# A state-space kernel matrix is stored and read back as a Toeplitz matrix: from the SyncE queue to GpSimd

## The chip, the cores and the metric

One core of a Trainium2 chip runs the whole program. The metric is the device time of one execution in microseconds (us); lower is better. All times come from runs on the chip and from one execution that the hardware profiler recorded.

## What is computed

The program is one inference step of a two-layer trunk over 264 tokens (256 of a prompt, 8 single-token samples), with shared weights, in f32. Each layer joins three branches fed by one projection: an S5 state space, a retention branch with a 128 x 256 state for each head and sample, and a convolution. A feed-forward part follows: dense in layer 0, eight experts in layer 1.

```python
z = u @ w_in
s5_out, s5_re, s5_im = s5_branch(z[..., OFF_S5:OFF_Q], ...)      # h = lbar*h + bbar*u ; y = Re(C h) + D u
ret_out, ret_state   = retention_branch(...)
conv_out, conv_state = conv_branch(...)
merged = gate_a*(s5_out @ s5_proj) + gate_b*(ret_out @ ret_proj) + gate_c*(conv_out @ conv_proj)
x = x + merged @ w_out
x = x + swiglu(rmsnorm(x))          # layer 0;  layer 1: top 2 of 8 experts
```

## The kernel before

**How the S5 part is done.** The 256 prompt tokens are cut into 32 chunks of S = 8. Inside a chunk the recurrence is a fixed 8 x 8 block-Toeplitz matrix of 16 x 16 blocks for each of 32 groups. TensorE makes the eight different blocks (tiles `kk`), ScalarE copies them into 16 partitions of `s5m` (L1263), and VectorE adds the skip term (L1758, semaphore `kmat_ready`). To become Toeplitz, these 16 partitions are stored to a scratch tensor in HBM, `kscr` (L618, 256 KB), and read back eight times, each time shifted by one block, into another 16 partitions of `s5m` (L624, 8 x 256 KB, semaphore `toep_in`). The tiles `y` (L910, L914) read the matrix. Before them TensorE waits for `h_ready`, which VectorE gives at the end of the sweep over the 32 chunks (L1674 to L1680), and for `toep_in` (L902).

**How weights arrive.** Dense weights come in chunks of 512 KB (eight 128 x 128 blocks) into a ring of five slots. SyncE (SP) issues them in order (L595); chunk n waits until TensorE is done with chunk n - 5. ScalarE makes the high part of a chunk (L1150), VectorE the low part (L1518), and TensorE uses three matmuls for each block (L684 to L686). ScalarE and VectorE do this up to two chunks ahead, but in program order with their other work: `full(key)` first splits the chunks up to the key's own plus two, and only then waits for the key.

**The order around the change.** On TensorE: gates `gg` 0 and 1, transposes `win`, `kk`, `si`, sample state 0, then `gg` 2 to 7 with the sample states 1, 2 and 3 behind `gg` 3, 4 and 6, then `y`, `gs` 0, sample state 4. In layer 0 `gg` 2 to 7 use chunks 30 to 35, `gs` 0 and 1 use 36 and 37 (layer 1: 182 to 187, 188 and 189). VectorE's update of sample state 3 stands behind the low part of chunk 36 (layer 1: 188), and the last step of the sweep behind that update. On SP the store and the eight loads stand between the issues of chunks 34 and 35 (layer 1: 186 and 187): SP waits for `kmat_ready`, stores, waits until the store has landed, issues the eight loads, and goes on to chunk 35.

**GpSimd (POOL)** makes the powers of the state matrix (`turns`, up to L2236) and then, for the sample states 0 to 7, waits for VectorE's update and stores the state (L2240, 512 KB). Between these it loads the states 4 to 7 (L2245). GpSimd's DMAs run on a queue of their own (q0, software), SP's on q1 (hardware).

Of the kernel before, what the change touches and what calls it, by code (L numbers as in the profile page):

```python
# [29 lines left out]
DEPTH = 2  # L30
G = 32
GP = 16
GJ = G // 2
S = 8
# [14 lines left out]
RING = 5  # L49
# [160 lines left out]
def chunk_of_tile():  # L210

    last, b = {}, 0
    for key, blocks in tile_order():
        b += blocks
        last[key] = (b + CH - 1) // CH - 1
    return last
# [13 lines left out]
def build(nc, a):  # L230
# [13 lines left out]
    CHUNK_OF = chunk_of_tile()  # L244
    PART = part_order()

    with ExitStack() as ctx:
        start_of = {}

        def sb(name, shape, dt=F):  # L250
            start_of[name] = -(-nc.sbuf_base // 32) * 32
            return ctx.enter_context(nc.sbuf_tensor(name, shape, dt))
# [6 lines left out]
        def sem(name):  # L259
            return ctx.enter_context(nc.semaphore(name))  # L260
# [6 lines left out]
        s5m = sb("s5m", [P, 15648])  # L267
# [147 lines left out]
        def weights(c, of):  # L415

            s = c % RING
            return of[:, s * CH * P:(s + 1) * CH * P]
# [10 lines left out]
        def slot(c, of):  # L429

            s = c % MRING
            return of[:, s * 2048:(s + 1) * 2048]
# [17 lines left out]
        kscr = nc.dram_tensor("kscr", [GP, (2 * S - 1) * G * GP], F, kind="Internal").ap()  # L450
# [28 lines left out]
        kmat_ready = sem("kmat_ready")  # L479
        dd_ready = sem("dd_ready")  # L480
        kscr_out = sem("kscr_out")
        toep_in = sem("toep_in")
        bc_in = sem("bc_in")
        zero_out = sem("zero_out")
# [55 lines left out]
        def out_of(key):  # L540

            return evicted[PLACE[key] % NBANK], PLACE[key] // NBANK + 1
# [33 lines left out]
        @block.sync  # L576
        def _(sp):
            sp.dma_start(lam[:, :, :], a["lam"]).then_inc(lam_in, 16)
            sp.dma_start(xT[:, :, :], a["xT"]).then_inc(x_in, 16)
            for n in range(2):  # L580
                sp.dma_start(weights(n, ring), a["weights"][n]).then_inc(loaded[n], 16)
            loads = [(vecs[:, :], a["vecs"]), (kdec[:, :, :], a["kdec"]),
                     (ident[:, :], a["ident"]), (tri[:, :], a["tri"]), (iota[:, :], a["iota"]),
                     (dskip[:, :, :], a["dskip"]), (router[:, :, :], a["router"])]
            for dst, src in loads:
                sp.dma_start(dst, src).then_inc(consts_in, 16)
            sp.dma_start(rope, a["rope"]).then_inc(table_in, 16)


            zg = zscr.rearrange("(g p) t -> p g t", p=GP)  # L590
            for n in range(2, N_CHUNKS):
                if n >= RING:

                    sp.wait_ge(mm_done, CHUNK_DONE[n - RING])
                sp.dma_start(weights(n, ring), a["weights"][n]).then_inc(loaded[n % RING], 16)  # L595
                for l in range(DEPTH):
                    if n == CHUNK_OF[(l, "v", 3)] + RING:

                        sp.wait_ge(*out_of((l, "k", 3)))
                        sp.dma_start(decay, a["decay"]).then_inc(table_in, 16)  # L600
                for l in range(DEPTH):
                    step = n - RING - CHUNK_OF[(l, "k", 0)]
                    if step == 0:

                        sp.wait_ge(zscr_out, 16 * (l + 1))
                        sp.wait_ge(xin_zero, 1)
                    if 0 <= step < S // 2:
                        for i in (2 * step, 2 * step + 1):
                            sp.dma_start(xin[i * GP:(i + 1) * GP, :, 0:NC], zg[:, :, i * NC:(i + 1) * NC]).then_inc(xin_in, 16)
                    if step == S // 2:  # L610
                        sp.dma_start(xin[0:GP, :, NC:NC + NS], zg[:, :, SEQ:T]).then_inc(xin_in, 16)
                        sp.dma_start(xin[P - GP:P, :, NC + NS:NC + 2 * NS], zg[:, :, SEQ:T]).then_inc(xin_in, 16)
                for l in range(DEPTH):
                    if n == CHUNK_OF[(l, "gg", 1)] + RING:

                        before = (S - 1) * G * GP
                        sp.wait_ge(kmat_ready, l + 1)
                        sp.dma_start(kscr[:, before:before + S * G * GP], s5m[0:GP, 0:S * G * GP]).then_inc(kscr_out, 16)  # L618
                        sp.wait_ge(kscr_out, 16 * (l + 1))
                        if l == 0:  # L620
                            sp.wait_ge(zero_out, 16)
                        for s in range(S):
                            lo = (S - 1 - s) * G * GP
                            sp.dma_start(s5m[s * GP:(s + 1) * GP, 0:S * G * GP], kscr[:, lo:lo + S * G * GP]).then_inc(toep_in, 16)  # L624
                if n == CHUNK_OF[(0, "gl", 0)] + RING:

                    sp.wait_ge(h_ready, 1)
                    sp.dma_start(rope, a["rope"]).then_inc(table_in, 16)


            sp.wait_ge(mm_done, DONE[(DEPTH - 1, "ps", KD - 1)])
            sp.wait_ge(merged, 16 * (DEPTH - 1) + KD)
            sp.wait_ge(hstate_out, 32 * DEPTH)
            for s in range(MRING):
                sp.dma_start(slot(s, s5m), a["experts"][s]).then_inc(mloaded[s], 16)
            l = DEPTH - 1
            sp.wait_ge(mm_done, DONE[(l, "xt", 5)])
            sp.dma_start(g_fin, a["gfin"]).then_inc(g_fin_in, 16)
            for i in range(3):
                lo, n = UT[i]  # L640
                n += CAP * (i == 2)
                sp.wait_ge(u_tok_ready, i + 1)
                sp.dma_start(u_rows[lo:lo + n, :], utok[0:n, i, :]).then_inc(u_rows_in, 16)
            sp.wait_ge(items_ready, 1)
            items = sp.value_load(items_t[0:1, 0:1], min_val=NEXP, max_val=3 * NEXP)
            with sp.Fori(0, items * TURNS - 1) as q:
                for s in range(MRING):

                    sp.wait_ge(mm_done, q * MRING + MM_BASE + s + 1)
                    row = ((q + 1) % (NEXP * TURNS)) * MRING + s  # L650
                    sp.dma_start(slot(s, s5m), a["experts"][bass.ds(row, 1)].rearrange("o p x -> (o p) x")
                                 ).then_inc(mloaded[s], 16)

            for s in range(AHEAD):
                sp.wait_ge(mm_done, items * E_CHUNKS + MM_BASE - MRING + s + 1)
                sp.dma_start(slot(s, s5m), a["experts"][s]).then_inc(mloaded[s], 16)


            sp.wait_ge(rows_added, items * 16 + 48)
            for i in range(3):  # L660
                lo, n = UT[i]
                sp.dma_start(xfin[0:n, i, :], x_rows[lo:lo + n, :]).then_inc(x_back[i], 16)
            for i in range(3):
                lo, n = UT[i]
                sp.wait_ge(x_final, i + 1)
                sp.dma_start(a["y"][lo:lo + n, :], xfin[0:n, i, :]).then_inc(y_out, 16)
            sp.wait_ge(y_out, 48)
# [1441 lines left out]
        def _(pool):  # L2109
# [36 lines left out]
            before = (S - 1) * G * GP  # L2146
# [6 lines left out]
            for l in range(DEPTH):  # L2153
# [74 lines left out]
                def more_turns(n):  # L2228

                    product([turns[:, r, :, n:2 * n] for r in range(2)], [turns[:, r, :, 0:n] for r in range(2)],  # L2230
                            [turns[:, r, :, n - 1:n].broadcast_to([P, GJ, n]) for r in range(2)], spare[:, :, 0:n])

                first_turns()
                for n in (1, 2, 4, 8, 16):
                    more_turns(n)
                pool.tensor_copy(spare[:, 0:1, 0:1], damp[:, 0:1].unsqueeze(2)).then_inc(turns_ready, 1)  # L2236
                for b in range(NS):
                    pool.wait_ge(*out_of((l, "oa", b)))
                    pool.wait_ge(*out_of((l, "ob", b)))
                    pool.dma_start(a["ret_s"][l, b], states[b % 4]).then_inc(s_out[b % 4], 16)  # L2240
                    if 1 <= b <= 4:
                        c = b - 1
                        pool.wait_ge(mm_done, DONE[(l, "os", c)])
                        pool.wait_ge(s_out[c], 16 * (2 * l + 1))
                        pool.dma_start(states[c], a["sret"][l, c + 4]).then_inc(s_in[c], 16)  # L2245
# [20 lines left out]
            for i in range(3):  # L2266
                lo, n = UT[i]
# [162 lines left out]
```

## Time and profile before

| what | us |
|---|---|
| three timed runs | 1957.0, 1957.76, 1958.45 (median 1957.76) |
| span of the profiled execution | 1954.9 |
| busy: TensorE | 1848.1 (95%) |
| busy: VectorE | 1544.7 (79%) |
| busy: ScalarE | 1195.4 (61%) |
| busy: GpSimd | 347.2 (18%) |
| moved by DMA | 527.5 MB, 270 GB/s in the mean |

Busy times are those of the profiled execution. Its program spans 1954.9 us; some 2.9 us of the timed median lie around the span. A busy TensorE is not TensorE at full rate: the granted clock says how fast it ran.

### The profile page before, as it was taken

The numbers are of one execution on the slowest core, as the hardware profiler recorded it, in microseconds if no ns is written. First come the engines' busy times: TensorE is split into PE (matmuls) and PEld (weight loads), VectorE is DVE, ScalarE is ACT, GpSimd is POOL, SyncE is SP. The second block draws the span as 40 slices with busy tenths as digits, with TensorE's granted clock in tenths as the row PEclk, the third lists the DMA queues.
The fourth block names the chain that finished last, engine by engine and source line by source line (L and its number), as shares of the span: only waits on it lengthen the run. The fifth ranks groups of instructions, "written<-read, shape, count | busy, mean of one in ns | idle before, by whom it ended". The sixth has DMA issues, their size and how long they took to land.

```text
span 1954.9 us, 31463 instructions
## 1 busy us (share of the span) xinstructions
PE 1848.1 (95%) x11751; PEld 1559.0 (80%) x11751; DVE 1544.7 (79%) x1758; ACT 1195.4 (61%) x1274; POOL 347.2 (18%) x449
## 2 busy tenths in 40 slices
PE   7788989899998998999899999999999999999995
PEld 6687889899998987999577777777777777777774
DVE  6986887666646967875699888898888988888886
ACT  4235545454434455454677777777777777777765
POOL 7974100069900030000000000000000000000000
PEclk8999999999999998999899999999999999999998
DMA  5447554455554656546599999999999999999996
GB/s 188 138 151 187 185 173 153 161 176 184 177 191 160 206 103 216 188 153 242 203 372 375 379 363 364 364 364 380 372 368 362 364 390 356 372 363 363 389 356 243
DMA packets 106786, 527.50 MB, mean 270 GB/s; under 512 B 22103, under 2 KB 23543, under 8 KB 62743
## 3 DMA queue, kind: packets, MB, share of 16 engines
q1 hardware_dynamic: 97303, 494.52, 69.6%
q0 software_dynamic: 8336, 30.63, 5.2%
q8 instruction: 63, 1.03, 0.2%
q10 hardware_dynamic: 1056, 1.08, 0.2%
q14 instruction: 28, 0.23, 0.0%
HBM read 505.69 MB, written 20.50 MB: 269 GB/s over the span
## 4 chain that ended last, share of the span: by engine, by line
PE 52%; DVE 4%; issue 3%; ACT 3%; DMA 2%; DVEq 0%; ACTq 0%; POOL 0%; POOLq 0%
PE bank L684 16%; PE bank L686 16%; PE bank L685 16%; DVE s5m_parts L2049 2%; PE bank L1091 1%; ACT zone_parts L1451 1%; DMA ring<-in_weights 1%; PE bank L1036 1%; DVE ring_parts L1518 0%; PE bank L717 0%; DMA s5m<-in_experts 0%; DVE s5m L1538 0%; PE bank L1123 0%; DMA x_rows<-work 0%; DVE zone L1649 0%
## 5 line engine op out<-in xcount | busy, mean ns | idle before, releaser
L2049 DVE TENSOR_TENSOR s5m_parts<-s5m,ring_parts 128x2048 fp32r<-128x2048 f32 x228 | 519.3, 2286 | 71.7 <-ACT ring_parts L1451 70.2
L1451 ACT ACTIVATE ring_parts<-s5m 128x2048 fp32r<-128x2048 f32 x228 | 432.2, 1917 | 89.5 <-DMA s5m<-in_experts 89.2
L1518 DVE TENSOR_TENSOR ring_parts<-ring,ring_parts 128x1024 fp32r<-128x1024 f32 x238 | 312.4, 1319 | 179.5 <-ACT ring_parts L1150 178.7
L684 PE MATMUL bank<-uT_parts,ring_parts 128*128 128x264 f32 x1312 | 386.9, 295 | 52.7 <-DVE ring_parts L1518 36.6
L685 PE MATMUL bank<-uT_hi,ring_parts 128*128 128x264 f32 x1312 | 380.6, 290 | 0.0
L686 PE MATMUL bank<-uT_hi,ring_parts 128*128 128x264 f32 x1312 | 379.9, 290 | 0.0
L1150 ACT ACTIVATE ring_parts<-ring 128x1024 fp32r<-128x1024 f32 x238 | 250.9, 1056 | 203.5 <-PE bank L686 151.5
L684 PE MATMUL bank<-s5m_parts,work_parts 128*112 128x512 f32 x896 | 359.1, 401 | 2.1 <-DVE table_parts L2041 2.0
L684 PEld LDWEIGHTS bank<-uT_parts,ring_parts 128*128 128x128 f32 x1312 | 255.5, 195 | 60.2 <-issue 58.9
L2049 DVE TENSOR_TENSOR s5m_parts<-s5m,zone_parts 128x2048 fp32r<-128x2048 f32 x112 | 255.6, 2287 | 52.9 <-ACT zone_parts L1451 52.7
L685 PEld LDWEIGHTS bank<-uT_hi,ring_parts 128*128 128x128 f32 x1312 | 256.5, 195 | 0.2
L686 PEld LDWEIGHTS bank<-uT_hi,ring_parts 128*128 128x128 f32 x1312 | 254.9, 194 | 0.0
L686 PE MATMUL bank<-ring_parts,work_parts 128*112 128x512 f32 x640 | 254.0, 397 | 0.0
L685 PE MATMUL bank<-ring_parts,table_parts 128*112 128x512 f32 x640 | 253.2, 396 | 0.0
L1451 ACT ACTIVATE zone_parts<-s5m 128x2048 fp32r<-128x2048 f32 x112 | 213.4, 1915 | 30.4 <-DMA s5m<-in_experts 28.0
L684 PEld LDWEIGHTS bank<-s5m_parts,work_parts 128*112 128x112 f32 x896 | 156.6, 175 | 51.6 <-issue 2.1
L684 PE MATMUL bank<-s5m_parts,zone_parts 128*112 128x512 f32 x448 | 177.1, 395 | 0.0
L684 PE MATMUL bank<-zone_parts,ring_parts 128*128 128x264 f32 x496 | 144.5, 291 | 2.6 <-DVE ring_parts L1518 2.1
L686 PEld LDWEIGHTS bank<-ring_parts,work_parts 128*112 128x112 f32 x640 | 112.0, 175 | 37.1
L685 PEld LDWEIGHTS bank<-ring_parts,table_parts 128*112 128x112 f32 x640 | 112.9, 176 | 35.9
L2288 POOL TENSOR_TENSOR work<-work 128x1 f32<-128x1 f32 x8 | 15.7, 1961 | 549.8 <-ACT work L1488 275.9
L1649 DVE SCALAR_TENSOR_TENSOR zone<-zone,vecs 128x256 f32<-128x256 f32 x240 | 109.3, 518 | 0.2
(349 smaller groups left out, 3031.6 us busy)
## 6 DMA issues: line engine op xcount, KB each, us to landing
s5m<-in_experts SPq DMA_DIRECT2D x340, 1024.0 KB, 6.7
ring<-in_weights SPq DMA_DIRECT2D x238, 512.0 KB, 3.3
work<-in_sret POOLq DMA_DIRECT2D x8, 512.0 KB, 6.1
zone<-in_sret POOLq DMA_DIRECT2D x8, 512.0 KB, 4.8
s5m<-kscr SPq DMA_DIRECT2D x16, 256.0 KB, 11.2
out_ret_s<-work POOLq DMA_DIRECT2D x8, 512.0 KB, 7.0
out_ret_s<-zone POOLq DMA_DIRECT2D x8, 512.0 KB, 4.0
xT<-in_xT SPq DMA_DIRECT2D x1, 1056.0 KB, 5.4
```

Of the source, the lines that this page charges most:

```text
L684: pe.matmul(out, left[0], right[1], start=first, stop=False)
L685: pe.matmul(out, left[1], right[0], start=False, stop=False)
L686: return pe.matmul(out, left[0], right[0], start=False, stop=last)
L1036: mm = pe.matmul(bank[2 + 2 * half][0:CAP, :], sel_first[0:n, i, :], xtok[i][0:n, half * WIDE:(half + 1) * WIDE], start=(i == 0), stop=(i ...
L1091: mm = pe.transpose(bank[b][:, x * CAP:(x + 1) * CAP], hm[0:CAP, t % 2, x * P:(x + 1) * P], ident[0:CAP, 0:CAP])
L1150: act.activation(weights_hi(c), weights(c, ring), ACT.Copy).then_inc(high_done, 1)
L1451: act.activation(high_slot(c), slot(c, s5m), ACT.Copy).then_inc(high_done, 1)
L1518: dve.tensor_tensor(weights(c, ring_parts), weights(c, ring), f32(weights_hi(c)), ALU.subtract).then_inc(low_done, 1)
L1649: dve.scalar_tensor_tensor(out=cT[:, m, 0:SEQ], in0=xc[:, m, k:k + SEQ], scalar=vec(l, V_DWW, m * TAPS + k), in1=cT[:, m, 0:SEQ], op0=ALU. ...
L2049: dve.tensor_tensor(slot(c, s5m_parts), slot(c, s5m), f32(high_slot(c)), ALU.subtract).then_inc(low_done, 1)
L2288: pool.tensor_tensor(turn[:, 0:1], turn[:, 1:2], turn[:, 2:3], ALU.add).then_inc(pool_turn, 1)
```

## The change

The two DMA groups leave the SP queue and go to GpSimd. The store comes right after the powers are done, before the loop over sample states. The eight loads stand inside the loop, after the store of sample state 0; GpSimd waits there until the kernels' store has landed. The wait on `zero_out` is not repeated, since GpSimd waits for it at its start.

```diff
@@ block.sync
-                for l in range(DEPTH):
-                    if n == CHUNK_OF[(l, "gg", 1)] + RING:
-
-                        before = (S - 1) * G * GP
-                        sp.wait_ge(kmat_ready, l + 1)
-                        sp.dma_start(kscr[:, before:before + S * G * GP], s5m[0:GP, 0:S * G * GP]).then_inc(kscr_out, 16)
-                        sp.wait_ge(kscr_out, 16 * (l + 1))
-                        if l == 0:
-                            sp.wait_ge(zero_out, 16)
-                        for s in range(S):
-                            lo = (S - 1 - s) * G * GP
-                            sp.dma_start(s5m[s * GP:(s + 1) * GP, 0:S * G * GP], kscr[:, lo:lo + S * G * GP]).then_inc(toep_in, 16)
@@ block.gpsimd
                 pool.tensor_copy(spare[:, 0:1, 0:1], damp[:, 0:1].unsqueeze(2)).then_inc(turns_ready, 1)
+                pool.wait_ge(kmat_ready, l + 1)
+                pool.dma_start(kscr[:, before:before + S * G * GP], s5m[0:GP, 0:S * G * GP]).then_inc(kscr_out, 16)
                 for b in range(NS):
                     pool.wait_ge(*out_of((l, "oa", b)))
                     pool.wait_ge(*out_of((l, "ob", b)))
                     pool.dma_start(a["ret_s"][l, b], states[b % 4]).then_inc(s_out[b % 4], 16)
+                    if b == 0:
+                        pool.wait_ge(kscr_out, 16 * (l + 1))
+                        for s in range(S):
+                            lo = (S - 1 - s) * G * GP
+                            pool.dma_start(s5m[s * GP:(s + 1) * GP, 0:S * G * GP], kscr[:, lo:lo + S * G * GP]).then_inc(toep_in, 16)
                     if 1 <= b <= 4:
```

## Rows read from the trace of the kernel before

**Rows 1.** What TensorE waited for, 140 to 240 us: total, times, longest.

```profile
PE bank L684 <- DVE ring_parts L1518: 5.1, 1, 5.1
```

**Rows 2.** The same, 690 to 790 us.

```profile
PE bank L684 <- DVE ring_parts L1518: 6.0, 1, 6.0
```

**Rows 3.** TensorE in order of time: start, duration, what, [idle before <- releaser].

```profile
185.88 0.74 PE L891 MATMUL bank<-work_parts 72*128 72x256 f32 x4
191.69 0.56 PE L684 MATMUL bank<-uT_parts,ring_parts 128*128 128x264 f32 x1 [5.07 <-DVE ring_parts L1518]
...
197.18 0.64 PE L910 MATMUL bank<-s5m 128*40 128x128 f32 x8
...
218.12 0.28 PE L684 MATMUL bank<-s5m_parts,ring_parts 128*128 128x264 f32 x1
...
746.83 0.64 PE L910 MATMUL bank<-s5m 128*40 128x128 f32 x8
```

**Rows 4.** ScalarE in order of time, from 180 us.

```profile
189.14 1.06 ACT L1150 ACTIVATE ring_parts<-ring 128x1024 fp32r<-128x1024 f32 x1 [8.79 <-DMA ring<-in_weights]
```

**Rows 5.** The SP queue in order of time, both layers.

```profile
163.95 0.34 SPq L618 DMA_DIRECT2D kscr<-s5m  x1
167.79 4.30 SPq L624 DMA_DIRECT2D s5m<-kscr  x8
172.14 49.45 SPq L595 DMA_DIRECT2D ring<-in_weights  x9
...
716.44 5.68 SPq L624 DMA_DIRECT2D s5m<-kscr  x8
722.16 0.90 SPq L595 DMA_DIRECT2D ring<-in_weights  x2
```

**Rows 6.** DMAs issued in 172.1:172.3, 171.95:172 and 720.3:722; last number us to landing.

```profile
ring<-in_weights SPq DMA_DIRECT2D x1, 512.0 KB, 17.0
...
s5m<-kscr SPq DMA_DIRECT2D x1, 256.0 KB, 15.2
...
s5m<-kscr SPq DMA_DIRECT2D x1, 256.0 KB, 16.2
```

**Rows 7.** Queue (packets, MB, share of 16 engines): 172:174 q0 and q1, 178:180 q1.

```profile
q0 software_dynamic: 108, 0.42, 68.7%
q1 hardware_dynamic: 22, 0.16, 28.5%
...
q1 hardware_dynamic: 32, 0.26, 97.6%
```

**Rows 8.** GpSimd in order of time, both layers.

```profile
166.23 0.19 POOL L2236 COPY sq<-rstd 128x1 f32<-128x1 f32 x1
168.18 0.60 POOL L2240 DMA_DIRECT2D out_ret_s<-work  x1 [1.77 <-DVE work L1798]
177.24 0.54 POOL L2240 DMA_DIRECT2D out_ret_s<-work  x1 [8.46 <-DVE work L1798]
...
714.86 0.19 POOL L2236 COPY sq<-rstd 128x1 f32<-128x1 f32 x1
```

**Rows 9.** Page, DMA issues: KB each and median us to landing.

```profile
kscr<-s5m SPq DMA_DIRECT2D x2, 256.0 KB, 3.8
...
kscr<-s5m POOLq DMA_DIRECT2D x1, 224.0 KB, 6.2
```

**Rows 10.** VectorE in order of time, layer 0.

```profile
193.85 1.41 DVE L1798 SCALAR_TENSOR_TENSOR zone<-zone,bank 128x256 f32<-128x256 f32 x4
...
196.44 0.18 DVE L1679 TENSOR_TENSOR hfin<-s5m,rstd 128x16 f32<-128x16 f32 x1
...
214.70 0.43 DVE L1535 TENSOR_TENSOR s5m_parts<-s5m,s5m_parts 128x264 fp32r<-128x264 f32 x1 [2.30 <-ACT s5m_parts L1164]
```

**Rows 11.** Stretch, PE, PEld, DVE, ACT, POOL busy (x), PEclk, DMA share, GB/s.

```profile
191.50:196.90 5.40, 5.21 (x24) 5.24 (x24) 4.24 (x11) 3.00 (x4) 1.47 (x3) 0.50 1.01 412
197.00:206.30 9.30, 9.30 (x194) 6.10 (x193) 8.68 (x23) 2.76 (x5) 0.04 (x1) 1.00 0.51 178
```

## The prediction

> **What bounds the kernel now.** I began with the page's shares: TensorE is busy 95% of the span, so only time in which TensorE waits, or runs at the lower clock, can be won. Next I asked what TensorE waits for around the lines that the change moves. Each layer has one long wait there, 5.1 us in layer 0 and 6.0 us in layer 1 [rows 1, 2], both for the low part of a weight chunk (L1518). The order of time places it: it is the first matmul of gate `gg` 7, at 191.69, after sample state 3 at 185.88 [rows 3]. ScalarE, a step earlier, had waited 8.79 us for that chunk's DMA [rows 4]. The SP queue tells why the DMA was late: in layer 0 the store of the S5 kernels goes out at 163.95, the eight Toeplitz loads from 167.79 to 172.09, and only then chunk 35, at 172.14 [rows 5]. That chunk takes 17.0 us to land, the last Toeplitz load 15.2 us from about 171.7 and in layer 1 16.2 us from about 720.3 [rows 6]. So the loads end near 186.9 and 736.5, and the chunk behind them lands at 189.1.
>
> The queues' shares show the rate of the loads. In 178 to 180 q1 moves 0.26 MB in 32 packets (16 of data, 16 small), at 97.6% of the engines' time [rows 7]: one Toeplitz load of 0.26 MB takes 2.0 us, eight take 16 us, at 131 GB/s. With ordinary traffic the same engines move 412 GB/s [rows 11], which is 1.3 us for 0.52 MB. The loads are therefore the expensive transfer, and they stand ahead of chunks 35 and 36. Chunk 36 matters too: VectorE updates sample state 3 only after its low part, at 193.85, and the sweep's end, on which `y` waits, follows at 196.62 [rows 10].
>
> **What the change removes.** From SP: one wait, a store, a second wait, eight issues. Chunk 35 no longer waits for them. TensorE is done with chunk 30 (`gg` 2) at about 170.5, counted as eight blocks of 24 matmuls after the first of `gg` 2, so its issue moves from 172.14 to 170.5. In layer 1 it moves from 722.16 to about 719.4. These 1.6 and 2.8 us are the smaller part. The larger is that it is now ahead of the Toeplitz loads.
>
> **What it adds on GpSimd.** The powers end at 166.42 and 715.05 [rows 8]. `kmat_ready` is there by then, since SP's store left at 163.95 [rows 5], so this wait costs nothing. The store takes 3.8 us from SP and 6.2 us from GpSimd, the latter in the crowded first microseconds with 224 KB [rows 9]; I take 4.8, nearer to SP's because the queues are as empty here, and keep both ends. GpSimd stores sample state 0 in between, at 168.18 as before, because VectorE releases it only then. The loads start at 166.42 + 4.8 = 171.2 instead of 167.8 in layer 0, and at 715.05 + 4.8 = 719.9 instead of 716.44 in layer 1. Eight issues of GpSimd at 0.60 us are 4.8 us, until 176.0; the next thing on GpSimd, the store of state 1, is released at 177.24 [rows 8], so nobody waits behind them. The later state stores and loads now stand behind the Toeplitz loads on q0. State 1 landed around 191 before and will land 2 or 3 us later. It gates a load of a state that is used some 20 us after that, so it costs nothing; if that cover were gone, the price would be those 2 to 3 us.
>
> **How long the loads take.** Before, from the first issue to the last landing: 186.9 - 167.8 = 19.1 us in layer 0 and 736.5 - 716.4 = 20.1 us in layer 1. In each there was one other transfer of 512 KB in the middle, the store of state 0: it is the 0.42 MB of q0 in 172 to 174, while q1 moved 0.16 MB [rows 7]. After the change chunk 36 takes this place (issued at about 173.5, when three or four loads are out), so I keep 19.1 and 20.1. The loads end at 171.2 + 19.1 = 190.3 and at 719.9 + 20.1 = 740.0. Chunk 35, issued at 170.5, and the store of state 0, at 168.2, come ahead of them and are 2.6 us of traffic at 412 GB/s.
>
> **What is late next.** Without the wait for chunk 35, `gg` 7 starts at 186.6 and lasts 24 x 0.122 = 2.9 us, where it took 5.2 us at a granted clock of 0.50 [rows 11], that is 1.2 GHz, after the idle time. It ends at 189.5. VectorE's update and the sweep's end take 2.8 us from 193.85 to 196.62 [rows 10]; begun at 186.6 they end at 189.4. The Toeplitz loads end last, at 190.3. With 0.2 us for the semaphore `y` starts at 190.5 instead of 197.18 [rows 3]: 6.7 us won. In layer 1 state 3 starts at 734.6, so `gg` 7 ends at 738.3, the loads at 740.0, and `y` starts at 740.2 instead of 746.83: 6.6 us won. Against this stands the clock. `y` ran at 1.00 [rows 11], right after a gate that had brought the clock back; now it follows 1 to 2 us of idle TensorE. That costs nothing if the clock stays, and at most some 2.5 us in each layer if `y` runs its first 5 us at half clock, as the gate did after 5.1 us of idleness. An idle time of 1 to 2 us is far shorter; I take 0.5 for each.
>
> Does the gain last to the end? After `y`, TensorE's next partner is VectorE's low part of the GELU output, begun at 214.70 after 2.30 us of idleness, and its matmul follows at 218.12 [rows 3, 10]. VectorE's own chain now starts with chunk 37, which lands right behind the Toeplitz loads, some 3.5 us earlier than before instead of 6.7; those 2.3 us and the 3 us before the matmul cover it. Later waits of TensorE follow from its own pace, so they shift.
>
> The sum is 6.7 + 6.6 - 1.0 = 12.3 us: the profiled 1954.9 becomes 1942.6, and the median 1957.76, which is 2.9 above the span, becomes 1945.5.
>
> **A rule against this change.** In the 178 to 186 stretch q0 had the store of state 1 waiting (issued 177.24 [rows 8]), and the row for 178 to 180 has q1 alone [rows 7]; no packet of q0 appears. The Trainium skill, DMA: Bandwidth & Descriptors, section Queues, rings and completion order, says that each DMA engine takes turns between the queues that have work, packet by packet. By it state 1 should have moved then, so this trace disagrees in that stretch; if the rule held after the change, rival A below would follow. The same page, section Issuing engines are not separate DMA queues, says that issuing from several engines only saves the issuer's time; by it the result would be rival B.
>
> **The rivals.**
> A: turns. Each engine gives one Toeplitz packet of about 2 us for each weight packet. Chunk 36 needs eight packets on each engine, so eight turns of 2.2 us, 17.6 us: it lands at 173.5 + 17.6 = 191.1, as late as now. Then its two parts, 2.3 us, the update and the sweep, 2.8 us, and `y` starts near 196.4; in layer 1 near 745. Gain 0.8 + 1.8 = 2.6: 1955.2. For it: 16-KB packets share engines with 4-KB ones. Against it: 172 to 174, where 108 packets of q0 passed against 22 of q1 [rows 7].
> B: the traffic of the loads stays in front of the chunks whoever issues them, and only the 1.6 and 2.8 us of earlier issue are won: 4.4 us, 1953.4. Against it: chunk 35 goes out before the first load.
> C: the loads are early enough (the store lands in 3.8 us, the loads run without a gap), and `gg` 7 and the sweep set the start of `y`: 197.18 - 189.5 = 7.7 and 746.83 - 738.3 = 8.5, together 16.2: 1941.6.
> D, slower: the loads cost more from GpSimd. Place: `toep_in` at `y`. If the store takes 6.2 (+1.4), two more chunks pass in front (+2.6) and each load takes 3.0 instead of 2.0 us (+8), `y` starts 12.0 us after my forecast of 190.5 and 740.2, so 5.3 and 5.4 us later than now: 1957.8 + 10.7 = 1968.5. It becomes a loss once a load takes longer than about 2.8 us, with nothing else late. For it: the trace of before has no 16-partition load from GpSimd. Against it: GpSimd's store of the zeros, of the same row form, was not slow for its place.
>
> **How the numbers follow.** Forecast 0.65, A 0.09, B 0.06, C 0.09, D 0.11. Around the forecast, 3.8 or 6.2 for the store moves each layer by 1.0 down or 1.4 up, one chunk more in front 1.3 up, the clock 0.5 down or 2 up: 1942 to 1952 for the forecast alone. The range reaches down to C and up to A: 1940.5 to 1955.5. A measurement of this kernel tells 0.2%, 3.9 us, from no change. Faster by more: forecast, C and half of B with a little lost at the edge, 0.77. Within: A, and half of B, 0.12. Slower: 0.11.
>
> **What would show it.** Right, if chunk 35's DMA lands within about 4 us, the 5.1 and 6.0 us waits at `gg` 7 are gone, `gg` 7 takes 2.9 us, and TensorE waits 1 to 2 us at L910 for the last Toeplitz load at about 190 and 740. Wrong, if ScalarE still waits for chunk 36 (A), if L910 doesn't wait at all (C), or if L910 waits over 6 us (D). The forecast hangs most on the 2.0 us of a load, which I carry over from SP's queue to GpSimd's.

## The result

The changed kernel is slower: 1964.2 us in the median of four runs against 1957.4 us for the kernel before; the ratio is 1.0048, with a 95% interval of 1.0034 to 1.0063. The loss is small, under 0.5%, but clear of the noise. Its profiled execution spans 1961.9 us against 1954.9. In that profile busy TensorE time is 1849.2 us, against 1848.1; the loss is not in work but in waiting and in the clock.

What TensorE waited for in the changed kernel, first 140 to 240 us, then 690 to 790 us (total, times, longest):

```profile
PE bank L898 <- DVE hfin L1667: 9.8, 1, 9.8
...
PE bank L898 <- issue: 7.4, 1, 7.4
```

The waits of 5.1 and 6.0 us at `gg` 7 [rows 1, 2] are gone, as forecast (0.35 us is left there). In their place TensorE waits 9.8 and 7.4 us one step later, at the first matmul of `y` (L898 here, L910 before). TensorE of the changed kernel in order of time:

```profile
187.31 0.36 PE L672 MATMUL bank<-uT_parts,ring_parts 128*128 128x264 f32 x1 [0.35 <-DVE ring_parts L1506]
...
200.24 1.08 PE L898 MATMUL bank<-s5m 128*40 128x128 f32 x8 [9.79 <-DVE hfin L1667]
...
211.13 0.39 PE L672 MATMUL bank<-uT_parts,ring_parts 128*128 128x264 f32 x1
...
224.16 0.42 PE L672 MATMUL bank<-s5m_parts,ring_parts 128*128 128x264 f32 x1
...
751.68 1.08 PE L898 MATMUL bank<-s5m 128*40 128x128 f32 x8 [7.45 <-issue]
...
763.22 0.39 PE L672 MATMUL bank<-uT_parts,ring_parts 128*128 128x264 f32 x1
```

In these lines `<-issue` means that the profile shows no releaser among the engines; in layer 1 it is the last Toeplitz load, which lands at 751.6. `y` starts at 200.24 where it started at 197.18, and eight of its matmuls take 1.08 us where they took 0.64 [rows 3]. Who is late? ScalarE, VectorE and GpSimd in layer 0:

```profile
195.18 1.06 ACT L1138 ACTIVATE ring_parts<-ring 128x1024 fp32r<-128x1024 f32 x1 [11.91 <-DMA ring<-in_weights]
...
197.41 1.41 DVE L1786 SCALAR_TENSOR_TENSOR zone<-zone,bank 128x256 f32<-128x256 f32 x4
...
200.01 0.18 DVE L1667 TENSOR_TENSOR hfin<-s5m,rstd 128x16 f32<-128x16 f32 x1
...
166.77 0.55 POOL L2226 DMA_DIRECT2D kscr<-s5m  x1
...
171.61 3.83 POOL L2235 DMA_DIRECT2D s5m<-kscr  x8 [2.51 <-DMA kscr<-s5m]
```

ScalarE waits 11.91 us for the DMA of chunk 36, where it waited 8.79 us for chunk 35 before [rows 4]. VectorE's update of sample state 3 and the end of the sweep follow at 197.41 and 200.19, which were at 193.85 and 196.62 [rows 10]. How long two transfers took (issued at 174.0 on SP's queue, at about 175.0 on GpSimd's; last number us to landing), and then the queues in 178 to 180 and 182 to 184:

```profile
ring<-in_weights SPq DMA_DIRECT2D x1, 512.0 KB, 21.2
...
s5m<-kscr POOLq DMA_DIRECT2D x1, 256.0 KB, 20.4
...
q0 software_dynamic: 34, 0.28, 95.7%
...
q0 software_dynamic: 25, 0.25, 92.3%
q1 hardware_dynamic: 21, 0.09, 30.0%
```

Chunk 36 lands at 195.2 and the last Toeplitz load at 195.3. The chunk is not served in one piece between two loads: while the loads run, q1 moves nothing at all in 178 to 180 and 21 packets of 4 KB in 182 to 184. The loads' queue moves 25 there, of which 10 are under 512 B, so some 15 rows of 16 KB.

The clock in three stretches of 5 us (columns as in [rows 11]):

```profile
195.00:200.00 5.00, 0.00 (x0) 0.00 (x0) 3.73 (x8) 3.28 (x5) 1.07 (x2) 0.50 1.03 419
200.00:205.00 5.00, 4.76 (x64) 3.03 (x68) 4.69 (x14) 0.00 (x0) 0.54 (x1) 0.58 0.87 324
...
220.00:225.00 5.00, 5.00 (x26) 5.00 (x26) 2.44 (x4) 4.03 (x10) 0.00 (x0) 0.53 0.39 120
```

During the idle time the granted clock falls to 0.50 (1.2 GHz) and `y` begins there. The last stretch lies mostly in `gs` 1, which ends at the first matmul on the GELU output (224.16). So the 7.0 us of span come together: 0.3 us were there before the stretch; `y` starts 2.7 us later beyond these (200.24 - 197.18 - 0.3); it lasts 10.9 us to 211.13 instead of some 9.2 (+1.7); from there to the first matmul on the GELU output, 224.16 here and 218.12 before [rows 3], another 1.3 us are lost: there the clock is 0.76 in the mean instead of 0.85. That is 6.0 us in layer 0. Between the layers 0.9 us more are lost (the powers of layer 1 end at 721.97 instead of 715.05 [rows 8], 6.9 us later). In layer 1 `y` starts 4.85 us later than before on the chip's time, which is 2.1 us earlier against the shift of 6.9, but it lasts 11.5 us instead of 9.2: the gain is spent on the clock.

### The profile page after: what moved, and what is told of

It reads as the page before. It is cut to its first block, busy times and chain, and to the rows that moved or that the text cites. A ratio compares the mean times of both kernels' runs of the same rounds, so it can differ in the third digit from the quotient of the medians.

```text
span 1961.9 us, 31462 instructions
## 1 busy us (share of the span) xinstructions
PE 1849.2 (94%) x11751; PEld 1558.4 (79%) x11751; DVE 1545.7 (79%) x1758; ACT 1194.9 (61%) x1274; POOL 356.3 (18%) x467
## 3 DMA queue, kind: packets, MB, share of 16 engines
q10 hardware_dynamic: 1056, 1.08, 0.2%
## 4 chain that ended last, share of the span: by engine, by line
PE 52%; DVE 4%; issue 3%; ACT 3%; DMA 2%; DVEq 0%; ACTq 0%; POOL 0%; POOLq 0%; SPq 0%
PE bank L672 16%; PE bank L674 16%; PE bank L673 16%; DVE s5m_parts L2037 2%; PE bank L1079 1%; DMA ring<-in_weights 1%; ACT zone_parts L1439 1%; DMA s5m<-in_experts 1%; PE bank L1024 1%; DVE ring_parts L1506 0%; PE bank L705 0%; DVE s5m L1526 0%; PE bank L1111 0%; PE bank L898 0%; PE bank L902 0%
## 5 line engine op out<-in xcount | busy, mean ns | idle before, releaser
L1463 ACT ACTIVATE s5m<-bank 112x512 f32<-112x512 f32 x56 | 33.6, 599 | 127.4 <-PE bank L674 127.4
```

Source lines behind the costliest of these rows:

```text
L1463: act.activation(hm[0:CAP, t % 2, :], bank[t % 2][0:CAP, :], ACT.Silu).then_inc(evicted[t % 2], 1)
```

## The experiments

The theory formed from these traces: while the loads and the weights stand in different queues, a 512-KB chunk gets through only in turns with the loads' long packets; the sweep waits for chunk 36 (188 in layer 1) and `y` waits for the sweep; and an idle TensorE begins `y` at half clock. The rivals: it only matters that the loads start 3.8 us later (rival 1), or GpSimd's software queue is slow at these rows (rival 2). The kernel before, run beside them, had medians of 1953.8 us for the first four experiments, 1955.5 for the next four and 1956.4 for the last four.

**The loads back on SP, behind chunk 35.**

```diff
-                            pool.dma_start(s5m[s * GP:(s + 1) * GP, 0:S * G * GP], kscr[:, lo:lo + S * G * GP])...
+                    if n == CHUNK_OF[(l, "gg", 1)] + RING + 1:
+                        sp.wait_ge(kscr_out, 16 * (l + 1))
+                        for s in range(S): ... sp.dma_start(...).then_inc(toep_in, 16)
```

> The store stays on GpSimd as after the change; the eight loads go back to the SP queue, between chunks 35 and 36 (layer 1: 187 and 188), so they start when the changed kernel's loads start (about 171.6 us) but stand in the same queue as chunk 36. Theory (turns: chunk 36 on SP's queue gets one 4-KB packet for each 16-KB Toeplitz packet of the other queue, and VectorE's sweep waits for chunk 36): chunk 36 lands right behind the loads, at about 192 instead of 195.2, y starts at about 197 instead of 200.2 in layer 0; y still runs in part at half clock after some 7 us of idle TensorE; 1957 to 1961 us. Rival 1 (the loads merely start 3.8 us later than before, whatever queue they are in): as the changed kernel, 1964. Rival 2 (GpSimd's software queue is itself slow at these rows, the order does not matter): a load takes 2.0 us again and the loads end near 190, against 195.5 after the change; 1957 to 1961 too, so this run does not tell it from the theory.

Measured: 1965.2 us, ratio 1.0067 (1.0047 to 1.0087), the profiled span 1958.5. Sample state 3 stands 2.2 us earlier on this trace's time than in that of before (183.66 against 185.88), so 195.42 here is 197.6 there (197.18 in the kernel before):

```profile
195.42 1.08 PE L904 MATMUL bank<-s5m 128*40 128x128 f32 x8 [7.51 <-DVE hfin L1673]
...
190.36 1.06 ACT L1144 ACTIVATE ring_parts<-ring 128x1024 fp32r<-128x1024 f32 x1 [9.65 <-DMA ring<-in_weights]
```

The place of `y` is as the theory said (197), not that of the changed kernel. Chunk 36 lands 2.3 us behind the loads, which end 17.6 us after their first issue. In layer 1 it is not so: the loads take 20.4 us, TensorE waits 8.9 us for the sweep, and `y` starts 12.0 us after the start of `gg` 7, against 10.6 in the changed kernel. The time is above the range I gave and about what rival 1 forecast (1964). The four values spread from 1960.3 to 1966.6, and the profiled execution is the fastest of them, so its rows show the best case. This run therefore doesn't tell the theory from rival 1, and it does show that the same queue alone is no help: here chunk 36 stands behind the loads. The idle time is 7.5 us in layer 0 and `y` starts at half clock here too.

**Behind chunk 36.** The same edit with `+ 2`.

> As the run before, but the loads stand behind chunk 36 on the SP queue, so they start later still (about 174.3 us in layer 0). Theory: chunk 36 is early, VectorE's sweep ends at about 189.4, the loads end at about 192.5 and set the start of y at about 193 (layer 1: 741 against 746.8 before); y partly at half clock, some 2 us in each layer; about 1951 us. Rival 1 (the start of the loads is what counts): 2.5 us later than after the change in each layer, about 1969 us. Rival 2: about 1951 as well.

Measured: 1958.5 us, ratio 1.0030 (1.0017 to 1.0042).

```profile
190.55 0.17 DVE L1673 TENSOR_TENSOR hfin<-s5m,rstd 128x16 f32<-128x16 f32 x1
...
197.49 1.08 PE L904 MATMUL bank<-s5m 128*40 128x128 f32 x8 [7.32 <-issue]
```

The sweep ends at 190.7, 9.5 us earlier than after the change, because chunk 36 is ahead of the loads. That is the theory's first half. But `y` still waits, now for the loads: they took 23.3 us from the first issue at 174.08 to 197.4, not the 18 I had assumed, and the time is 7.5 us above the 1951 that I expected. Rival 1 falls: the loads start 2.5 us later than in the changed kernel, for which it forecast about 1969, and the kernel takes 1958.5. Its ratio is below that of the changed kernel (1.0030 against 1.0048), but the two intervals touch, so it is not shown to be faster than it.

**The loads cut to an eighth, on GpSimd.**

```diff
-dma_start(s5m[s * GP:(s + 1) * GP, 0:S * G * GP], kscr[:, lo:lo + S * G * GP])
+dma_start(s5m[s * GP:(s + 1) * GP, 0:G * GP], kscr[:, lo:lo + G * GP])
```

> The changed kernel with eight loads of 32 KB (one block of each row) instead of 256 KB; seven eighths of the Toeplitz matrix are left out, so y is computed from what stood in s5m. It shows what the waits, issues and places on GpSimd's queue cost without the traffic. Theory: nothing of the loss is in them; chunk 36 lands within 5 us, y starts at about 189.5 in layer 0 and 738.5 (before's clock) in layer 1 at full clock; about 1941 us. Rival 1 (place and time of the issue cost the time): stays above 1957.

This kernel leaves out seven eighths of the matrix. Measured: 1943.1 us, ratio 0.9948 (0.9927 to 0.9969).

```profile
190.53 0.64 PE L898 MATMUL bank<-s5m 128*40 128x128 f32 x8 [0.59 <-DVE hfin L1667]
```

So no loss is in the waits, issues and places on GpSimd; the whole matter is the traffic of 2 MB. With an eighth of it the kernel is 10.7 us faster than the one before. This is the floor for any placing of the loads, and it is less than the 12.3 us that I had forecast for the full traffic. In layer 1 `y` starts at 732.77, 14.1 us earlier than before, but the span is only 11.4 us shorter: 2.7 us of the gain don't reach the end.

**Half rows.**

```diff
+                            for half in range(2):
+                                c, w = half * (S // 2) * G * GP, (S // 2) * G * GP
+                                pool.dma_start(s5m[s * GP:(s + 1) * GP, c:c + w], kscr[:, lo + c:lo + c + w])...
```

> The changed kernel with each load cut into two of 8 KB for each partition, all data moved. Theory (turns by packets): a Toeplitz packet is half as long, so chunk 36 gets its turns twice as often and lands 10 to 12 us after its issue (about 185) instead of 21.2 us; the loads end at about 195 and set y; 1955 to 1960 us. Rival 1 and rival 2: as the changed kernel or slower by the eight more issues, 1964 or more, with chunk 36 as late as there.

Measured: 1959.6 us, ratio 1.0029 (1.0018 to 1.0041). Chunk 36 was issued at 172.54:

```profile
ring<-in_weights SPq DMA_DIRECT2D x1, 512.0 KB, 14.2
...
195.07 1.08 PE L898 MATMUL bank<-s5m 128*40 128x128 f32 x8 [6.06 <-issue]
```

The same bytes on the same queue in packets of half the length, and chunk 36 lands after 14.2 us instead of 21.2. That is what turns by packets foretell. The run leaves a rival, though: GpSimd issues the sixteen halves in 7.6 us instead of 3.8, so when chunk 36 is issued only about half as many bytes have been given to the other queue. No run tells the length of the packets from that. `y` then waits for the last load.

**ScalarE's hardware queue.**

```diff
+                act.wait_ge(kscr_out, 16 * (l + 1))
+                for s in range(S): ... act.dma_start(s5m[...], kscr[...]).then_inc(toep_in, 16)
```

> The store stays on GpSimd, the eight loads are issued by ScalarE (hardware queue q10) when the store has landed, at about the time of the changed kernel's loads; ScalarE stands still for some 8 us for it, with slack. Theory (turns between queues, whoever issues): chunk 36 on q1 is as late as after the change, 18 to 22 us from issue to landing, and y starts at about 200 in layer 0; 1960 to 1966 us. Rival 2 (GpSimd's software queue is what is slow): chunk 36 lands early or behind the loads at 192 at the latest, 1950 to 1957 us.

Measured: 1966.6 us, ratio 1.0056 (1.0036 to 1.0076). Chunk 36, issued at 172.38, took even a little longer than beside GpSimd's queue:

```profile
ring<-in_weights SPq DMA_DIRECT2D x1, 512.0 KB, 23.4
```

Rival 2 falls: chunk 36 is late beside any second queue that I tried, a software or a hardware queue, and the loads are no faster from ScalarE (27.4 us in layer 0, 22.6 in layer 1). The total time is a weaker witness: while ScalarE issues the loads (169.7 to 174.2), its own work stands still, and TensorE waits 2.6 and 2.3 us at the gates for weights, which it does not in the changed kernel.

**The sweep freed of chunk 36.** VectorE prepares only one chunk ahead before sample state 3.

```diff
-                        full(key)
+                        low_weights(CHUNK_OF[key] + (1 if b == 3 else 2))
+                        dve.wait_ge(mm_done, DONE[key])
```

> The changed kernel, but VectorE makes the low part of only one chunk ahead, not two, before it updates sample state 3, so the sweep no longer waits for chunk 36 (188). Theory (in layer 0 the sweep's wait for chunk 36 is what makes y late, the loads land at 195.5): h_ready comes at about 190, y starts at the last load, about 195.8 instead of 200.2, unless the bank of the second half of y, which waits for the same chunk through ScalarE, holds it; in layer 1 y starts at the loads anyway, no change. 1958 to 1962 us. Rival (the loads' own lateness is the cause, chunk 36 only stands beside it): no change from the changed kernel, 1964.

Measured: 1956.4 us, ratio 1.0003 (0.9987 to 1.0019), so better than expected and clearly apart from the changed kernel. Chunk 36 is as late as there (22.4 us), and yet:

```profile
188.43 0.18 DVE L1667 TENSOR_TENSOR hfin<-s5m,rstd 128x16 f32<-128x16 f32 x1
...
195.38 1.08 PE L898 MATMUL bank<-s5m 128*40 128x128 f32 x8 [6.18 <-issue]
```

Sample state 3 stands 0.9 us earlier here, so `y` starts at 196.3 on the time of before, 3.6 us earlier than in the changed kernel. That shows the chain chunk 36, sweep, `y` for layer 0. In layer 1, where I expected no change, `y` waits 4.6 us instead of 7.4: there the loads start 1.6 us earlier against `gg` 7 and take 23.4 us instead of 24.6. The edit explains neither, so part of this run's gain stays open.

**One load of 128 partitions, on SP and on GpSimd.** The store writes the blocks mirrored, so that one access pattern with positive steps names all eight shifted copies.

```diff
-                        for s in range(S): ... (eight loads)
+                        rows = bass.AP(tensor=kscr.tensor, offset=kscr.offset, ap=[[G * GP, S], [(2 * S - 1) * G * GP, GP], [1, S * G * GP]])
+                        sp.dma_start(s5m[:, 0:S * G * GP], rows).then_inc(toep_in, 16)
```

> The kernel before with its store and loads in their old place on SP, but one load of 128 partitions (2 MB) instead of eight of 16 partitions. For this the block order is mirrored (kernels, zeros, powers of C and the read-out of y), nothing is left out; GpSimd does nine small copies more in each layer. Theory (a 16-partition load is slow because all 16 engines write to the same few partitions; 131 GB/s against 412): 2 MB in 5 to 6 us, or 10 if only eight engines take part, so the load ends at about 175 to 179, chunk 35 lands by 180, no wait at gate 7, y at about 189.5 at full clock; as the run with small loads, 1941 to 1945 us (0.5% faster than before). Rival (it is the 16-KB rows that are slow, whatever the partitions): 16 us as before, about 1957.

> The same single load in the changed kernel's place on GpSimd, with its store there. Theory: the load is short enough that turns don't hurt, chunk 36 lands within 10 us of its issue, y at about 189.5 to 191; 1941 to 1946 us, so the place of the issue no longer matters within 2 us of the run with SP. Rival 2 (GpSimd's queue is slow): several us slower than on SP.

Measured: 1975.2 us, ratio 1.0095 (1.0071 to 1.0120) on SP; 1971.4 us, ratio 1.0083 (1.0064 to 1.0102) on GpSimd. Both expectations were wrong, by some 30 and 25 us. On SP chunk 35, behind the load, took 27.4 us to land, on GpSimd the load itself 29.6 us:

```profile
ring<-in_weights SPq DMA_DIRECT2D x1, 512.0 KB, 27.4
...
s5m<-kscr POOLq DMA_DIRECT2D x1, 2048.0 KB, 29.6
```

Fewer and larger loads were no help. The outermost size of this pattern is 8, and the trace of the SP run shows eight packets of 16 KB at a time. From 168.9 to 170.2, with hardly anything beside them:

```profile
q1 hardware_dynamic: 8, 0.13, 49.1%
```

Eight packets in 1.3 us fill half of the time of sixteen engines, so half of the engines carried this load. That left open what makes the rows of the eight small loads slow, where all sixteen are busy [rows 7], and two probes in the kernel before were to tell.

**Partitions or source.**

```diff
-sp.dma_start(s5m[s * GP:(s + 1) * GP, 0:S * G * GP], kscr[:, lo:lo + S * G * GP])
+sp.dma_start(s5m[s:P:S, 0:S * G * GP], kscr[:, lo:lo + S * G * GP])                              # first probe
+sp.dma_start(s5m[s * GP:(s + 1) * GP, ...], a["experts"][s, 0:2 * GP, :].rearrange(...))         # second probe
```

> A cost probe in the kernel before: each of the eight loads writes the same 16 rows of 16 KB to partitions eight apart instead of 16 neighbours; the matrix rows stand in the wrong places for y, so y is not the Toeplitz product. If the 16 neighbouring partitions limit a load (2.0 us for 256 KB), it now takes about half, and the last load lands about 10 us after the first issue instead of 19 to 20, and the wait at gate 7 goes: about 1945 us. If reading kscr from HBM is the limit, nothing changes: 131 GB/s, 19 us, 1957 us.

> The same probe from the other side: the eight loads write to the 16 neighbouring partitions as before but read 16 rows of 16 KB of the expert weights instead of kscr; the Toeplitz matrix is left out. If the partitions limit a load: 131 GB/s and 19 us as before, 1957 us. If the source limits it: near 400 GB/s, all loads landed within 8 us, about 1945 us.

The first probe puts the rows in the wrong places, the second leaves the matrix out. Measured, one run each: 1945.7 us with the spread partitions, 1960.1 us with the other source. The median us from issue to landing of a load, first probe, then second; it is 11.2 before:

```profile
s5m<-kscr SPq DMA_DIRECT2D x16, 256.0 KB, 6.3
...
s5m<-in_experts SPq DMA_DIRECT2D x16, 256.0 KB, 11.4
```

Another tensor in HBM as source makes no difference. Sixteen neighbouring partitions do: the same rows to partitions eight apart land in a median of 6.3 us instead of 11.2, the eight loads take 13.4 us in layer 0 instead of 19.1 (I had expected about 10), and the wait at `gg` 7 is gone. Why neighbouring partitions are slow, no run shows.

**Two versions that use what was found.** First: loads on SP behind chunk 35 and the sweep freed (the first and the sixth edit together).

> The store on GpSimd, the loads on SP behind chunk 35 (as in the first experiment), and VectorE's sweep freed of chunk 36 by one chunk less of looking ahead before sample state 3. Theory (after the change y waits first for chunk 36 by way of the sweep, then for the loads; both must be out of the way): gate 7 on time, h_ready at about 190, the last load lands 17.9 us after its first issue and sets y at about 190.5 instead of 197.2 in layer 0 and 741 instead of 746.8 in layer 1, short idle time; 1943 to 1950 us, 0.4 to 0.7% faster than before. Rival (the traffic of the loads costs the same wherever it stands): 1957.

Measured: 1947.7 us, ratio 0.9957 (0.9940 to 0.9973).

```profile
193.17 0.64 PE L904 MATMUL bank<-s5m 128*40 128x128 f32 x8 [3.52 <-issue]
...
194.63 1.08 PE L904 MATMUL bank<-s5m 128*40 128x128 f32 x8
```

`y` waits 3.5 us for the loads in layer 0 and not at all in layer 1. In layer 0 it begins at full clock, but its next eight matmuls of this form take 1.08 us: the granted clock is 0.53 in 194.4 to 197.5, and `y` lasts 10.7 us against 9.2 in layer 1. The loads took 22.4 us in layer 0 and 17.6 in layer 1, in the same place of the queue. Second: one load, with channel outside and step inside, for the inputs, the input matrix and the Toeplitz matrix alike.

```diff
-        gb = s5m[:, 0:4096].rearrange("p (j r s q) -> p j r s q", ...)
+        gb = s5m[:, 0:4096].rearrange("p (j r q s) -> p j r s q", ...)
-                            sp.dma_start(xin[i * GP:(i + 1) * GP, :, 0:NC], ...)
+                            sp.dma_start(xin[i:P:S, :, 0:NC], ...)
+ap=[[(2 * S - 1) * G * GP, GP], [G * GP, S], [1, S * G * GP]]
```

> The kernel before with the loads in their old place on SP, as one load of 2 MB whose 128 partitions are ordered with the channel outside and the step inside (S5 inputs, input matrix and Toeplitz matrix all in this order, block order mirrored as in the earlier single-load runs), so that 16 engines take part and they write to partitions eight apart; nothing is left out. Theory (neighbouring partitions are the limit, and the earlier single load used eight engines): 2 MB in 8 to 10 us, landed by 178; chunk 35 lands by about 180, y at about 189.5 at full clock; 1941 to 1946 us, 0.6 to 0.8% faster than before. Rival (kscr's HBM is the limit): 16 us or more, 1957 or slower.

Measured: 1945.6 us, ratio 0.9948 (0.9931 to 0.9964).

```profile
s5m<-kscr SPq DMA_DIRECT2D x1, 2048.0 KB, 12.2
...
q1 hardware_dynamic: 32, 0.52, 119.2%
...
192.76 0.64 PE L910 MATMUL bank<-s5m 128*40 128x128 f32 x8 [0.59 <-DVE hfin L1679]
```

The 2 MB land 12.2 us after their issue (13.0 in layer 1), more than the 8 to 10 I expected, and early enough. In 172 to 174 q1 moves 32 packets, 16 in a microsecond instead of 6 in the run with an outermost size of 8. And `y` waits 0.6 us, at full clock. It reaches the floor of the run with the small loads (ratio 0.9948 both times). All data is moved and nothing left out, so this version beats both kernels, by 0.52% and, the two ratios set against each other, about 1%.

## Why the prediction was wrong

Point by point:

- **What bounds the kernel now** was right: the 5.1 and 6.0 us at `gg` 7 came from the loads ahead of chunk 35, and they vanished.
- **GpSimd's side** was right: the store took 4.6 us against my 4.8, the loads started at 171.61 against 171.2, nobody waited behind them, and the run with small loads shows the places cost nothing.
- **How long the loads take** is the step that failed. I carried the 19.1 and 20.1 us of before over and let chunk 36 "take this place", that is, be served in one piece between two loads, as the store of state 0 had been. It took 21.2 us to land. The loads took 171.61 to 195.3, 23.7 us, in layer 0 and 24.6 us in layer 1, some 3.0 us for each load instead of 2.4 or 2.5. The ScalarE run shows that chunk 36's lateness goes with any second queue; the half-row run fits turns by packets, with the rival named there.
- **What is late next** failed with it: I named the loads, at 190.3; in layer 0 it was the sweep, at 200.2, by way of chunk 36, and in layer 1 the loads, at 751.6, with the sweep 1.1 us ahead of them.
- **The clock** was mis-sized. I took 0.5 us for each layer with 1 to 2 us of idle time. The idle times were 9.8 and 7.4 us, `y` lost 1.7 and 2.3 us, and the stretch up to the GELU output 1.3 us more in layer 0. The trace of before had a warning: after 2.9 us of idleness the clock stood at 0.50 from 166.4 to 169.7.
- **Whether the gain lasts** was taken for granted. With the small loads 2.7 of 14.1 us didn't reach the end; in the last version all of its 11.1 us did. Why, no run shows. The 2.9 us between span and median also seem 1 us too many: in each later run the time is some 1.8 us above its own span.
- **Rival A** was the right mechanism, with a chance of 0.09 and a price too low: it put chunk 36 at 191.1 and `y` at 196.4, still a gain of 2.6. With the measured 195.2 and the clock the same mechanism is a loss. I weighed 172 to 174 against it, where 108 packets of q0 passed against 22 of q1 [rows 7]; the store of state 0 had been issued when one Toeplitz load was out, and chunk 36 when five were. That difference may be why it was no model for chunk 36; no run tests it.
- **The slower rival** put the cost in the loads' price on GpSimd. Its 3.0 us for each load came true in size (23.7 us for eight), but from ScalarE's queue the loads are as slow and chunk 36 as late, so its reason was wrong, though it lies on the right side; it had chunk 36 and the sweep not in it at all.

On the rule against this change: the Trainium skill, DMA: Bandwidth & Descriptors, section Queues, rings and completion order, has each engine take turns between queues by packets; its packet is a bundle, typically 9 to 17 descriptors, while the packets that the profile counts here are single rows of 4 or 16 KB. In the changed kernel 182 to 184 agrees in that both queues move (21 against 25 packets), 178 to 180 does not (34 against none). Why the second queue gets nothing in some stretches and turns in others stays open. So does how long eight loads last in one queue: behind chunk 35 on SP they took 17.6 and 20.4 us in one run and 22.4 and 17.6 in the other, behind chunk 36 23.3 and 21.4.

## What to carry to other kernels

Before a transfer moves to another queue, ask what stands beside it there and how long its packets are: in one queue the order of issue protects what is urgent, if it is issued first; in two queues an urgent transfer of short packets was held up beside long ones: it took 21.2 us to land, against 4.8 beside the small loads. Look then at who reads ahead of need: here a sweep waited for a weight chunk it did not use. And ask first why the transfer is long; 2 MB that took 19 us took 12 as one load in another order of partitions, and then nothing waited for it even in its old place.

## What the runs showed of the hardware

- DMAs from HBM to 16 neighbouring partitions moved 131 GB/s in rows of 16 KB [rows 7], and were as slow from another tensor (median landing time 11.4 us against 11.2); the same rows to partitions eight apart had a median landing time of 6.3 us instead of 11.2, when several were queued. A single pattern of 2 MB took 12.2 us with an outermost size of 16 and partitions eight apart, and 29.6 us (on GpSimd's queue) with an outermost size of 8 and neighbouring partitions. No run changes only one of the two in a single load; the packets took about as long in both (1.2 and 1.3 us, from the lines shown), but 16 ran at a time in the first and 8 in the second.
- After 4.6 us of idle TensorE and more, `y` began at half clock (eight matmuls in 1.08 us). After 3.5 us it began at full clock (0.64 us) and fell to half clock soon after (0.53 in 194.4 to 197.5); after 0.6 us it kept the full clock.
- Idleness is not needed for it. In the kernel before the clock was 0.51 in 214.2 to 217.6, with TensorE busy all the time, soon after 2.99 us of small transposes (L927, 40x40).
